# Product-key top-k of a two-block layer: expert indices matched in 16-bit floats, both halves in one pass, six more dots beside it

## The reference, cut to what matters

```python
def peer_ffn(h, wq, sub_keys, expert_u, expert_v):
    def block(xb):
        q = (xb @ wq).reshape(PEER_BLOCK, PEER_HEADS, 2, PEER_HALF)
        s = jnp.einsum('thpd,hpkd->thpk', q, sub_keys).astype(jnp.float32)
        s_top, i_top = lax.top_k(s, PEER_TOPK)
        cand_s = (s_top[:, :, 0, :, None] + s_top[:, :, 1, None, :]).reshape(...)
        cand_i = (i_top[:, :, 0, :, None] * PEER_N_KEYS + i_top[:, :, 1, None, :]).reshape(...)
        best_s, best_pos = lax.top_k(cand_s, PEER_TOPK)
        experts = jnp.take_along_axis(cand_i, best_pos, axis=-1)
        g = jax.nn.softmax(best_s, axis=-1)
        act = jax.nn.gelu(jnp.einsum('thkd,td->thk', expert_u[experts], xb).astype(jnp.float32))
        wgt = (g * act).astype(xb.dtype)
        return jnp.einsum('thk,thkd->td', wgt, expert_v[experts])
```

## Time and profile before

| | us |
|---|---|
| median of 3 runs | 2431.11 (2428.7 to 2432.45) |
| the profiled execution | 2430.69 |
| its span in the trace | 2428.8 |
| TensorE busy | 2371.3 |
| VectorE busy | 1581.1 |
| GpSimd busy | 1261.2 |
| ScalarE busy | 946.3 |

### The profile page before, as it was taken

The page is one execution under the profiler, slowest core; times in us unless marked ns, Lnnn a source line. Parts: engine busy times, 40 slices in busy tenths (PEclk is TensorE's granted clock), DMA queues, the critical chain, the costliest instruction groups (busy, mean ns, idle before and its releaser), DMA issues.

```text
span 2428.8 us, 35950 instructions
## 1 busy us (share of the span) xinstructions
PE 2371.3 (98%) x12892; PEld 2127.6 (88%) x12892; DVE 1581.1 (65%) x2823; ACT 946.3 (39%) x1488; POOL 1261.2 (52%) x704
## 2 busy tenths in 40 slices
PE   7999999999999999999999999999999999999998
PEld 4878887899999999999999999997777888888886
DVE  5258435789989999689999999993267225322201
ACT  4373333334455555333333333442353223332312
POOL 3305444337899999456556655454304444444443
PEclk9999999999999999999999999999999999999999
DMA  7227422337877888999999999953202322223231
GB/s 281 79 114 265 172 96 97 121 98 263 308 228 273 286 310 299 373 396 411 417 418 415 417 403 417 391 204 112 78 18 81 110 95 96 94 89 103 88 103 70
DMA packets 180765, 527.64 MB, mean 217 GB/s; under 512 B 18368, under 2 KB 72048, under 8 KB 179376
## 3 DMA queue, kind: packets, MB, share of 16 engines
q1 hardware_dynamic: 121504, 345.99, 39.5%
q0 software_dynamic: 43024, 159.14, 16.9%
q10 hardware_dynamic: 16128, 21.11, 2.4%
HBM read 475.68 MB, written 50.49 MB: 217 GB/s over the span
## 4 chain that ended last, share of the span: by engine, by line
PE 70%; DVE 17%; DMA 6%; issue 5%; ACT 1%; SPq 0%; POOL 0%; ACTq 0%; DVEq 0%; POOLq 0%
PE bank L1365 17%; PE bank L1366 17%; PE bank L1367 17%; DMA AJ<-act_dram 5%; PE pair L1366 3%; PE pair L1365 3%; PE pair L1367 3%; DVE YROW L2513 3%; DVE X L2289 3%; PE pair L1719 2%; DVE wlo L2445 2%; DVE WL L2482 1%; DVE AJ L2477 1%; DVE T L2357 1%; DVE T L2358 1%
## 5 line engine op out<-in xcount | busy, mean ns | idle before, releaser
L707 POOL TENSOR_TENSOR wlo<-wraw,whi 128x1024 fp32r<-128x1024 f32 x303 | 742.7, 2455 | 767.1 <-ACT whi L849 766.5
L1365 PE MATMUL bank<-HH,whi 128*128 128x512 f32 (+1 forms) x2048 | 741.2, 362 | 8.5 <-DMA T<-in_keys 2.9
L1366 PE MATMUL bank<-HL,whi 128*128 128x512 f32 (+1 forms) x2048 | 736.9, 360 | 0.0
L1367 PE MATMUL bank<-HH,wlo 128*128 128x512 f32 (+1 forms) x2048 | 736.5, 360 | 0.0
L849 ACT ACTIVATE whi<-wraw 128x1024 fp32r<-128x1024 f32 x456 | 481.1, 1056 | 506.5 <-PE bank L1367 215.0
L1365 PEld LDWEIGHTS bank<-HH,whi 128*128 128x128 f32 x2048 | 385.6, 188 | 54.4 <-issue 5.1
L1367 PEld LDWEIGHTS bank<-HH,wlo 128*128 128x128 f32 x2048 | 385.3, 188 | 40.2
L1366 PEld LDWEIGHTS bank<-HL,whi 128*128 128x128 f32 x2048 | 385.6, 188 | 39.5 <-issue 0.5
L773 POOL DMA_INDIRECT VROW<-in_w,which x128 | 211.1, 1649 | 181.2 <-DVE YROW L2513 165.1
L2445 DVE TENSOR_TENSOR wlo<-wraw,whi 128x1024 fp32r<-128x1024 f32 x153 | 186.6, 1220 | 21.8 <-ACT whi L849 21.8
L766 POOL DMA_INDIRECT X<-in_u_rows,which x128 | 156.3, 1221 | 62.1 <-DVE dots L2289 38.5
(11 more groups left out here) (443 smaller groups left out, 3857.7 us busy)
## 6 DMA issues: line engine op xcount, KB each, us to landing
wraw<-in_w SPq DMA_DIRECT2D x456, 512.0 KB, 4.4
gate_dram<-GS SPq DMA_DIRECT2D x24, 1024.0 KB, 10.8
GJ<-gate_dram SPq DMA_DIRECT2D x32, 768.0 KB, 11.7
act_dram<-actb ACTq DMA_DIRECT2D x112, 184.0 KB
AJ<-act_dram SPq DMA_DIRECT2D x112, 184.0 KB, 10.7
adaw<-in_ada SPq DMA_DIRECT2D x32, 512.0 KB, 6.0
ada<-in_ada SPq DMA_DIRECT2D x16, 512.0 KB, 14.0
NB<-in_nab POOLq DMA_DIRECT2D x4, 1024.0 KB, 5.8
```

Source lines behind the costliest of these rows:

```text
L707: nc.gpsimd.tensor_tensor(wlo[:, slot, :, :].rearrange("p k c -> p (k c)"), wraw[:, slot, :, :].rearrange("p k c -> p (k c)"), whi[:, slot ...
L1365: pe.matmul(out_, ah, bh, start=first, stop=False, **kw)
L1366: pe.matmul(out_, ah, bl, start=False, stop=False, **kw)
L1367: return pe.matmul(out_, al, bh, start=False, stop=last, **kw)
```

## The change

It replaces the lookup of the indices, moves dots, and reorders the fetches. The new lookup holds places (`place_at`), the numbers 0 to 15 (`place_of`) and the indices (`spread`) as 16-bit floats in SBUF and treats both halves at once: one comparison of 128x4096, one product of 128x4096, one addition that folds 16 places to 8 (2048 results) and two sums over 8 places. `spread` holds each index 16 times over; ScalarE writes it in eight parts, after eight of its U tiles between 3 and 16, from a float copy `list_index` that VectorE makes of `tki` once. VectorE waits for it by `index_spread`, and `tkf` is gone. The head maxima for `gsel` are copied to PSUM first (`top_value`). The two semaphores are two that the first stage had used.

```diff
-DOTS_TOP = (0, 6, 11, 11)
+DOTS_TOP = (0, 6, 14, 14)
+TURNS_TOP = 9
...
-U_DOTS = 96
+U_DOTS = 102
...
-V_DOT_TILES = [9 * m // 4 + 1 for m in range(48)][:DOTS - U_DOTS]
+V_DOT_TILES = [5 * m // 2 + 1 for m in range(42)][:DOTS - U_DOTS]
...
-                if t > 25 and fetched < R + TOP_DOTS and t % 4 == 0:
+                if t > 17 and fetched < R + TOP_DOTS and t % 3 == 0:
                     fetch_u(fetched)
                     fetched += 1
...
+            def spread_index():
+                n, w = spreads[0] // 2, spreads[0] % 2
+                spreads[0] += 1
+                if n == 0 and w == 0:
+                    act.wait_ge(list_known, 33)
+                index = list_index[:, ORDER[n], :, :].rearrange("p (h w) a -> p w h a", w=2)[:, w]
+                nc.scalar.activation(spread[:, n, w * NH:(w + 1) * NH, :, :], bc(index, 3, 16), ACT.Copy).then_inc(index_spread, 1)
...
+            spread_index()
             for i in range(1, LEAD_IT):
-                u_iteration(i)
+                u_iteration(i, ((0, 2), (0, 2), (0, 2), (0,))[i - 1] if i <= 4 else ())
...
-                    if turns[0] > 11 - DOTS_TOP[n]:
+                    late = TURNS_TOP - DOTS_TOP[n] if n == 1 else 0
+                    while dotted[0] < sum(DOTS_TOP[:n]) + DOTS_TOP[n] * max(turns[0] - late, 0) // (TURNS_TOP - late):
                         dot()
...
-                nc.vector.tensor_copy(tkf, tki[:, tb, :, :])
...
+                nc.vector.tensor_copy(top_value, bv[:, :, 0])
...
-                nc.vector.tensor_tensor(gsel[:, tb, :].rearrange("p (h k) -> p h k", h=NH), bv[:, :, :], bc(bv[:, :, 0], 2, 16),
+                nc.vector.tensor_tensor(gsel[:, tb, :].rearrange("p (h k) -> p h k", h=NH), bv[:, :, :], bc(top_value, 2, 16),
...
-                for w in range(2):
-                    settled(nc.vector.tensor_tensor(cand, bc(babf[:, w, :, :], 3, 16), iota16, ALU.is_equal))
-                    settled(nc.vector.tensor_tensor(cand, cand, bc(idx[:, w], 2, 16), ALU.mult))
-                    chosen = selj[:, tb, :] if w else seli[:, tb, :]
-                    settled(nc.vector.tensor_reduce(chosen.rearrange("p (h k) -> p h k", h=NH), cand, AX_X, ALU.add))
...
+                settled(nc.vector.tensor_tensor(picks, bc(place_at, 2, 16), bc(place_of, 1, 2 * NH), ALU.is_equal))
+                v.wait_ge(index_spread, 32 + 2 * (n + 1))
+                settled(nc.vector.tensor_tensor(picks, picks, spread[:, n], ALU.mult))
+                settled(nc.vector.tensor_tensor(picks[:, :, 0:8, :], picks[:, :, 0:8, :], picks[:, :, 8:16, :], ALU.add))
+                for w, chosen in enumerate((seli, selj)):
+                    ins = nc.vector.tensor_reduce(chosen[:, tb, :].rearrange("p (h k) -> p h k", h=NH),
+                                                  picks[:, w * NH:(w + 1) * NH, 0:8, :].rearrange("p h a k -> p h k a"), AX_X, ALU.add)
+                settled(ins)
...
+            nc.vector.tensor_copy(list_index, tki).then_inc(list_known, 1)
+            then(nc.vector.tensor_copy(place_of, bc(iota[:, 0:16], 2, 16)))
```

More of the change, by code:

```diff
@@ L252, in build @@
         keysT = T[:, 0:4, :].rearrange("p a b -> p (a b)").rearrange("p (n k) -> p n k", k=P)
-        cand = T[:, 0:4, :].rearrange("p a b -> p (a b)").rearrange("p (h a b) -> p h a b", h=NH, a=16)
+        picks = T[:, 0:4, :].rearrange("p a b -> p (a b)").bitcast(BF).rearrange("p (n a k) -> p n a k", n=16, a=16)
+        spread = GS[:, 0, :, :].rearrange("p a b -> p (a b)").bitcast(BF).rearrange("p (t n a k) -> p t n a k", t=TB, n=16, a=16)
+        list_index = GS[:, 1, 0:16, :].rearrange("p a b -> p (a b)").rearrange("p (t n a) -> p t n a", t=TB, n=16)
+        place_of = GS[:, 1, 16:18, :].rearrange("p a b -> p (a b)").bitcast(BF).rearrange("p (a k) -> p a k", k=16)
+        place_at = GS[:, 1, 18:20, :].rearrange("p a b -> p (a b)").bitcast(BF).rearrange("p (n k) -> p n k", k=16)
         small = T[:, 4:6, :].rearrange("p a b -> p (a b)").rearrange("p (t n a) -> p t n a", t=TB, n=16)
@@ L325, in build @@
         bank += [pair[b // 2][:, b % 2, :] for b in range(4)]
-        tkf = bank[6][:, 0:256].rearrange("p (n a) -> p n a", n=16)
+        top_value = bank[6][:, 0:NH]
         bab = bank[6][:, 256:512].bitcast(U32).rearrange("p (w h k) -> p w h k", w=2, h=NH)
@@ L351, in build @@
         ring_in = [sem(f"ring_in{s}") for s in range(R)]
-        ada1_in = [sem(f"ada1_in{a}" + ("_or_gates" if a < 2 else "_or_few" if a < 6 else "")) for a in range(8)]
+        ada1_in = [sem(f"ada1_in{a}" + ("_or_gates" if a < 2 else "_or_few" if a < 6 else "_or_spread")) for a in range(8)]
         gates_in = ada1_in[0:2]
         few_out, few_in, few_gate_out, few_gate_in = ada1_in[2:6]
+        list_known, index_spread = ada1_in[6:8]
         ada_used = sem("ada_used")
@@ L1063, in act_tile, with u_iteration @@
                 act.dma_start(act_dram[j, :, :], actb[:, u % 2, :]).then_inc(act_out[u % 2], 16)
-            def u_iteration(i):
+            def u_iteration(i, spread_at=()):
                 for u in range(4):
@@ L1068, in u_iteration @@
                     act_tile(i * 4 + u, u, i * 32 + 16 * (u // 2))
+                    if u in spread_at:
+                        spread_index()
+            spreads = [0]
+            def spread_index():
[5 more added lines that the diff above has]
+                nc.scalar.activation(spread[:, n, w * NH:(w + 1) * NH, :, :], bc(index, 3, 16), ACT.Copy).then_inc(index_spread, 1)
             def gate_exp(n):
@@ L2339, in topk @@
                 nc.vector.tensor_scalar(bab[:, 0, :, :], bp[:, :, :], 3, None, ALU.logical_shift_right)
-                nc.vector.tensor_scalar(bab[:, 1, :, :], bp[:, :, :], 7, None, ALU.bitwise_and)
-                nc.vector.tensor_tensor(gsel[:, tb, :].rearrange("p (h k) -> p h k", h=NH), bv[:, :, :], bc(bv[:, :, 0], 2, 16),
+                nc.vector.tensor_copy(top_value, bv[:, :, 0])
+                then(nc.vector.tensor_scalar(bab[:, 1, :, :], bp[:, :, :], 7, None, ALU.bitwise_and))
+                nc.vector.tensor_tensor(gsel[:, tb, :].rearrange("p (h k) -> p h k", h=NH), bv[:, :, :], bc(top_value, 2, 16),
                                         ALU.subtract).then_inc(tk_diff, 1)
@@ L2350, in topk @@
                 then(nc.vector.scalar_tensor_tensor(row, row, 1.0, beyond, ALU.max, ALU.add))
[L2351 to L2355, removed]
-                for w in range(2):
-                    settled(nc.vector.tensor_tensor(cand, bc(babf[:, w, :, :], 3, 16), iota16, ALU.is_equal))
-                    settled(nc.vector.tensor_tensor(cand, cand, bc(idx[:, w], 2, 16), ALU.mult))
-                    chosen = selj[:, tb, :] if w else seli[:, tb, :]
-                    settled(nc.vector.tensor_reduce(chosen.rearrange("p (h k) -> p h k", h=NH), cand, AX_X, ALU.add))
+                nc.vector.tensor_scalar(place_at[:, 0:NH, :], row, -1.0, None, ALU.add)
+                then(nc.vector.tensor_tensor(place_at[:, NH:2 * NH, :], place, wide, ALU.add))
+                settled(nc.vector.tensor_tensor(picks, bc(place_at, 2, 16), bc(place_of, 1, 2 * NH), ALU.is_equal))
[6 more added lines that the diff above has]
+                settled(ins)
             v.wait_ge(const2_in, 32)
```

## The result

The kernel after takes 2438.91 us (2437.22 to 2443.33), the kernel before, beside it, 2431.4 us (2428.19 to 2433.09): ratio 1.0032, 95% interval 1.0023 to 1.0040. It is 7.5 us slower. I had forecast no change, 2431.0 us; the time lies inside the range of 2419 to 2440, next to the rival "GpSimd starves TensorE, slower", which gave 2436.7.

What follows compares the result with a forecast made beforehand. TensorE, busy 2371.3 of 2428.8 us, was taken as the bound, with winnable time only at the top-k's gate and in the V stage. 2430.69 + 7.8 (gate) - 7.5 (V stage) gave 2431.0 us, range 2419 to 2440.

Steps and rivals of the forecast that it cites:

- GpSimd starves TensorE, slower: Rival in the top-k: b = 18, gate at 695.6, + 12.8; V gives 6.8; 2436.7 us; chance 0.19.
- The bottlenecks: TensorE lacks 3.1 of 81 us beside the top-k, with a lowered clock after it, and 9.9 of 430 in V.
- The V stage: From 1090 to 1520, six dots and six gathers leave: 7.5 us won, with ends of 4 and 9.9 us.
- The durations: Unheld top-k passes: about 2.2 us each for the long two, 1.1 the fold, sums 1.1 or twice that.
- What GpSimd loses: In the top-k, VectorE's two-SBUF-operand instructions delay GpSimd's `wlo` and fetches: 13 us taken, between 6.6 and 18.
- b: The time GpSimd loses to VectorE up to `wlo` 38 in the top-k, put at 13 us.
- `wlo` 38: GpSimd's `wlo` for U tile 38 ends at 668.3 + b; tile 38 forecast at 681.3 in place of 675.5.
- the 0.17 us: One matmul's time, by which TensorE was taken to begin tile 38 ahead of the row at 675.62.
- VectorE's own chain: In the top-k: lookup 7.7 us a round, VectorE's work down some 25 us, so something else ends the top-k.
- The end of the gate: After `wlo` 38: 0.2 issue, 6.2 landing, 1.1 dot, 1.8 softmax sum; gate at 690.6, 7.8 us later.
- The clock: TensorE's slow matmuls after the gate's idle time: 1.5 us lost, left as it was.
- The sum: Whole kernel: 2430.69 of the profiled execution, + 7.8 - 7.5, gives 2431.0 us.

Runs made afterwards that it cites:

- second profile: The unchanged kernel after, run and profiled once more: median 2439.63 us, ratio 1.0029 against the kernel before; the profiled execution took 2440.3 us.
- first profile after: The kernel after as first profiled: that execution took 2443.33 us, 4.4 above the median of 2438.91 us.
- kernel of 2423.31 us: Kernel before with its old lookup, head maxima and other second SBUF operands outside the lookup copied to PSUM, six dots moved: 2423.31 us, ratio 0.9964.

## Why the prediction was wrong, step by step

**The bottlenecks** were the right ones: the gate and the V stage hold all of the change.

**The V stage** was mis-sized: -7.5 us forecast. Over 1090 to 1520 TensorE lacks 3.7 to 6.1 us, 5.1 in the mean, in the seven profiles with six dots moved, and 9.0 to 10.4, 9.9 in the mean, in the four with none: -4.8 (unrounded, 9.93 - 5.08). I took a value near the prices of the work that goes; the low end, 4 us, was nearer. A reason that fits, but that no run tests: VectorE still waits for `AJ`, 16.4 us as before, now 10 times (16.6 us in the second profile), as the first profile after shows beside the wait that became less:

```profile
DVE AJ L2501 <- DMA AJ<-act_dram: 16.4, 10, 3.7
...
PE bank L1385 <- DVE WL L2506: 4.3, 5, 2.2
```

**The durations** of the unheld operations were right: 2.29 us for the 4096 16-bit elements, 1.21 for the fold, 0.29 for the gate difference. The trace agrees, with the 2.29, with the Trainium skill, page "VectorE: DVE Perf Modes", section on the perf-mode tier table, which gives a 16-bit `tensor_tensor` in SBUF twice the rate. The two sums took 2.1 us each, the other end that I had named.

**What GpSimd loses** was right: b was put at 13. In the second profile eleven fetches take 1.23 to 2.84 us, and together they lie 12.9 us over 0.95 each, 11.8 of these up to `wlo` 38; one `wlo` is held too, 3.36 in place of 2.41 us. The first fetch comes 1.0 us later than before, at 565.93, where I had taken 1.9. `wlo` 38 ended at 682.35, forecast 681.3. (TensorE began tile 38 with the row at 675.62 itself, 24 matmuls before the end of the tile, and not one matmul ahead of it; no term hangs on the 0.17 us.) What the Trainium skill, page "SBUF — State Buffer", section "Who interferes with whom", infers, that making descriptors escapes such a VectorE instruction, is not borne out: 2.82 in place of 0.95 us beside a product.

**VectorE's own chain** is the step that failed. I wrote that each pass first waits for a `wlo` and then GpSimd waits for the pass, but put only the second half into the sum. VectorE's account got 7.7 us a round for the lookup and, with the six dots already counted, some 25 us less work in all, from which followed that something else ends the top-k. The lookup in the second profile, 540 to 705 us (times, busy us, mean ns, idle before), and VectorE's wait for rows (total us, times, longest):

```profile
L2377 DVE TENSOR_TENSOR T<-T,GS 128x4096 bf16<-128x4096 bf16 x4 | 15.7, 3913 | 0.0
L2378 DVE TENSOR_TENSOR T<-T 128x2048 bf16<-128x2048 bf16 x4 | 13.1, 3276 | 0.0
L2375 DVE TENSOR_TENSOR T<-GS 128x4096 bf16<-128x4096 bf16 x4 | 11.3, 2834 | 0.1
L2380 DVE TENSOR_REDUCE seli<-T 128x128 f32<-128x1024 bf16 x4 | 8.5, 2130 | 0.0
L2380 DVE TENSOR_REDUCE selj<-T 128x128 f32<-128x1024 bf16 x4 | 8.4, 2094 | 0.0
...
DVE X L2309 <- DMA X<-in_u_rows,which: 7.8, 6, 3.0
```

The lookup takes 57.0 us in four rounds, 14.2 a round, more than the 54.8 of the 32-bit one. Of the 26 us above the forecast, 17 are waits (the three passes take 40.1 us, and 23.2 when nothing holds them) and 8 are the two sums, for which I took the lower of two values. The gate difference gives 8 us back, the six dots take 6.8. In all VectorE is busy for 154.7 us of the top-k (531.3 to 695.5) where it was 149.3 (531.9 to 682.8): 5 us more work, not 25 less. Besides, it waits 7.8 us for rows, which it did not do before. The two together are the 13 us by which the top-k lasts longer.

**The end of the gate** failed for that reason. Behind `wlo` 38 I counted 9.3 us: the issue, a landing, one dot, the softmax sum. It was 13.2 us (682.35 to 695.54), and no landing ends it: the rest of the fold, two dots, the two sums (4 us), two dots, and the softmax sum with its last product held. So the gate came 12.7 us later, not 7.8.

**The clock** I left as it was; it cost 1.2 us more, behind a standstill of 8.86 in place of 3.07 us.

**The sum**: +7.8 - 7.5 was forecast. The second profile's +13.9 at the gate and the -4.8 of the V stage make +9.1; its time lies 2440.3 - 2430.69 = 9.6 above that of before. The sum thus missed by 8.8 us: 4.9 at the gate, 1.2 of clock and 2.7 in the V stage. The medians differ by 6.7 to 7.5.

**The rival** that came true had the right sign and size by a different road: b = 18 was not needed, 13 and VectorE's own waits did it, and the V stage gave 4.8 where it had 6.8. That its time came so near is luck, and so is the time's place inside the stated range.

**The interaction** I had not seen: by the medians the lookup alone costs +0.4 us and the dots alone +1.7, neither clear of no change, and both together 7.5. To have the 16-bit lookup in place of the 32-bit one costs 5.5 us with the dots of before and only the head maxima in PSUM, and 12.7 with six dots moved and all the operands in PSUM, so these two pairs differ in more than the dots. That held fetches are cheap while few are wanted, and dear when six more dots want them sooner, would fit, but it is argued and not tested, and the one profile of the lookup alone does not bear it out: VectorE waits 8.2 us for rows there too. Why two parts that are nearly free cost 7.5 us together stays open.

## What to carry to other kernels

A wait between two engines has two sides, and both belong in the sum: what the waiting instruction adds to its own engine's chain, and what it holds up afterwards. Packing to 16 bits was worth nothing here, where it moved the second operand from PSUM to SBUF beside a busy GpSimd; a copy of a few columns into PSUM, 0.17 us for the head maxima, won 5.1 us. A step that loses alone and a step that gains alone have to be tried together, and so do two that are each nearly free.

## What the runs showed of the hardware

- A 16-bit pass over 4096 elements takes 2.29 us packed, 4.42 with one operand in PSUM as 32-bit floats, and 4.43 with one operand repeated in the innermost direction.
- A sum over 1024 16-bit elements takes 1.21 us from neighbours and 2.1 from elements 16 apart.
- A GpSimd indirect fetch is held by VectorE's instructions with two SBUF operands as a `wlo` is: 2.8 in place of 0.95 us beside a packed product, 4.95 beside an unpacked comparison. Where one operand of each was in PSUM, in the kernel of 2423.31 us, none of the 40 fetches between 560 and 715 us was lengthened (0.99 us at the most).
- After 8.86 us of standstill TensorE's transposes began at the lower level (0.21 us apart); after 3.07 they began at the higher one (0.11) and fell a little later.
